# Two weight blocks of the down product loaded behind the last unit's weights: a change in the order of one DMA queue

## What is computed

```
h2 = rms_norm(x, norm_mlp[layer])
x = x + jnp.square(jax.nn.relu(h2 @ w_ff1[layer])) @ w_ff2[layer]
return rms_norm(x, norm_final)
```

## Time and profile before

| | us |
|---|---|
| median of 3 runs | 1670.12 (1668.62 to 1670.35) |
| profiled execution, its time | 1671.03 |
| its span, first to last instruction | 1669.4 |
| TensorE busy | 1654.0 (99%) |
| VectorE busy | 1023.4 (61%) |
| ScalarE busy | 706.4 (42%) |

### The profile page before, as it was taken

One profiled execution on the slowest core, in us unless ns is written; L12 is line 12 of the kernel. 1 busy time (PEld: TensorE's weight loads), 2 busy tenths in 40 slices (PEclk: granted clock), 3 DMA queues, 4 the chain that ended last, 5 costly groups with the idle time before them and its releaser, 6 DMA issues.

```text
span 1669.4 us, 25092 instructions
## 1 busy us (share of the span) xinstructions
PE 1654.0 (99%) x10242; PEld 1244.0 (75%) x10242; DVE 1023.4 (61%) x1347; ACT 706.4 (42%) x891; POOL 111.0 (7%) x168
## 2 busy tenths in 40 slices
PE   9999999999999999999999999999999999999998
PEld 7898898864444535453588877778888889889986
DVE  6975668452242334324668755567675477878887
ACT  6565553321011101111366633444542367856775
POOL 4000000000000000000011022311000001000000
PEclk9999999999999999999999999999999999999999
DMA  7233224958999999999541331223253349767864
GB/s 266 64 116 111 76 77 151 389 207 344 428 429 428 429 428 428 429 428 428 203 153 55 101 101 57 72 77 128 102 178 104 111 132 261 162 177 224 205 140 125
DMA packets 92209, 355.65 MB, mean 213 GB/s; under 512 B 7936, under 2 KB 7952, under 8 KB 79824
## 3 DMA queue, kind: packets, MB, share of 16 engines
q1 hardware_dynamic: 79776, 328.04, 50.9%
q0 software_dynamic: 12336, 26.23, 8.1%
HBM read 347.97 MB, written 6.29 MB: 212 GB/s over the span
## 4 chain that ended last, share of the span: by engine, by line
PE 95%; DMA 2%; DVE 1%; ACT 1%; issue 1%; POOL 0%; DVEq 0%; ACTq 0%; POOLq 0%
PE bank L3424 35%; PE bank L3829 13%; PE bank L4281 9%; PE bank L3842 6%; PE bank L4256 6%; PE bank L3572 6%; PE bank L3736 4%; PE bank L3775 3%; PE bank L4012 2%; PE bank L3449 2%; DMA ring<-in_w 1%; PE bank L3470 1%; DMA stage<-in_w_ff 1%; PE bank L4042 1%; PE bank L4065 1%; PE bank L4112 1%
## 5 line engine op out<-in xcount | busy, mean ns | idle before, releaser
L3424 PE MATMUL bank<-act_hi,w_hi 128*128 128x512 f32 x608 | 240.3, 395 | 0.0
L3424 PE MATMUL bank<-act_hi,w_lo 128*128 128x512 f32 x608 | 236.8, 390 | 0.0
L3424 PE MATMUL bank<-act_lo,w_hi 128*128 128x512 f32 x608 | 236.8, 389 | 0.0
L3829 PE MATMUL bank<-ring,xgT 128*64 128x512 f32 x992 | 216.1, 592 | 1.6 <-DMA ring<-in_w 1.0
L3829 PEld LDWEIGHTS bank<-ring,xgT 128*64 128x64 f32 x992 | 71.9, 137 | 141.9 <-issue 139.6
L2238 DVE TENSOR_TENSOR w_lo<-w_stage,w_hi 128x2048 fp32r<-128x2048 f32 x55 | 126.0, 2291 | 83.0 <-ACT w_hi L1324 77.2
L1324 ACT ACTIVATE w_hi<-w_stage 128x2048 fp32r<-128x2048 f32 x53 | 101.7, 1919 | 152.0 <-PE bank L3424 143.3
L4281 PE MATMUL bank<-down,part_hi 128*128 128x512 f32 x448 | 138.2, 390 | 0.2 <-issue 0.2
L3424 PEld LDWEIGHTS bank<-act_hi,w_hi 128*128 128x128 f32 x608 | 114.2, 188 | 25.8 <-issue 2.9
L3424 PEld LDWEIGHTS bank<-act_hi,w_lo 128*128 128x128 f32 x608 | 114.1, 188 | 24.3
L3424 PEld LDWEIGHTS bank<-act_lo,w_hi 128*128 128x128 f32 x608 | 114.3, 188 | 22.7
(11 more groups left out here) (584 smaller groups left out, 3585.3 us busy)
## 6 DMA issues: line engine op xcount, KB each, us to landing
ring<-in_w SPq DMA_DIRECT2D x93, 2048.0 KB, 16.6
w_stage<-in_w_in SPq DMA_DIRECT2D x40, 1024.0 KB, 5.1
w_stage<-in_w_ff SPq DMA_DIRECT2D x19, 1024.0 KB, 6.8
b_sum<-in_w_ff POOLq DMA_DIRECT2D x12, 1024.0 KB, 11.9
w_stage<-in_w_out SPq DMA_DIRECT2D x8, 1024.0 KB, 5.1
b_one<-in_w_ff SPq DMA_DIRECT2D x6, 1024.0 KB, 7.4
stage<-in_w_ff SPq DMA_DIRECT2D x5, 1024.0 KB, 5.9
x_tm<-in_x SPq DMA_DIRECT2D x8, 512.0 KB, 8.8
```

Source lines behind the costliest of these rows:

```text
L3424: ins = pe.matmul(banks[j][:, :], left, right, start=(kc == 0 and k == 0 and n_pass == 0), stop=(kc == g.chunks - 1 and k == g.ktiles - 1 ...
L3829: ins = pe.matmul(dst[mine, :], xgT[:, 4 * kh + k, slots], up_weights(2 * w + kh, q, k, ahead), start=(kh == 0 and k == 0), stop=(kh == 1 ...
```

## The change

One call in SP's program, `load_ones(0)`, which issues the loads of `b_one[1]` and of `b_far` for the first half, moves from in front of both weight blocks of unit 3 to behind them:

```diff
             load_blocks(2, 1)
             unit_split(1)
-            load_ones(0)
             load_blocks(3, 0)
             third_made(2)
             load_blocks(3, 1)
+            load_ones(0)
             unit_split(2)
             load_step(0, 0)
```

## The result

The changed kernel takes 1683.21 us (median of 6 runs, 1682.2 to 1683.41), the kernel before 1669.72 us (6 runs, 1668.62 to 1670.35): 13.5 us more, a ratio of 1.0079 with a 95% interval of 1.0069 to 1.0089. The profiled execution has a span of 1680.6 us against 1669.4 us.

What follows compares the result with a forecast made beforehand. The prediction took TensorE, busy 1654.0 of 1669.4 us, as the bound. A removed wait, a new stop and a slower clock gave -0.9 + 12.3 + 2.2 = +13.6 us, so 1683.7 us, range 1677.5 to 1688.0.

Steps and rivals of the forecast that it cites:

- The wait that comes: At product (2, 4): ScalarE stands at b_one's negation and TensorE stops; +12.3 us, or 7.6 to 16.3 us by the bounds.
- 1.95 us to spare: Before the change, slack between the low part's end at 1396.98 and TensorE's start of product (2, 4) at 1398.93.
- The time to land: b_one's load, from its issue at 1395.00 to landing at about 1407: 12 us, bounds 7.3 and 16.0 us.
- The wait that goes: At product (3, 2): TensorE's late start from late block (3, 1) should go, with less loaded ahead; -0.9 us.
- I find no other gain: Beyond the 0.87 us at product (3, 2), nothing: down-phase transfers come later and TensorE shows no wait for them.
- The clock: After the stop, product (2, 4) should begin at half rate; +2.2 us, between nothing and 2.9 us.
- The long stop: Rival: b_one waits behind (3, 1) while a third addition takes its half; stop 16.3 us, time 1688.4 us; chance 10%.
- The short stop: Rival: b_one lands 7.3 to 9.6 us after issue; stop 7.6 to 9.9 us, time 1677.9 to 1681.1; chance 18%.
- The sum: Whole kernel: -0.9 + 12.3 + 2.2 = +13.6 us, against the median of 1670.12 us makes 1683.7 us.

Runs made afterwards that it cites:

- The base run: The changed kernel run again, unaltered, beside three further variants on the same chip: 1683.26 us, ratio 1.0074 to the kernel before.

## Why the prediction was right

- **The wait that comes.** The mechanism came as forecast, and so did its size. The prediction put b_one's issue 0.41 us behind block (3, 1), its landing 12 us later and the stop at 12.3 us. The trace has 0.41, 12.1 (1393.09 to 1405.2) and 12.64 us. Its chain from there is a little short: from ScalarE's start of the negation to TensorE's first multiplication it is 1409.66 - 1405.21 = 4.45 us, not 4.2, for between the low part's end at 1409.33 and the first multiplication lie 0.33 us, where 0.05 was taken for all hand-overs. The same 0.3 us is missing in the 1.95 us to spare; but ScalarE also stood 0.29 us behind the negation for W3, which is missing too, and the two cancel. The run with the negations later shows that this stop is the whole cause, and the run with b_one alone that this load is.
- **The time to land.** That it took 12 us is a hit with luck in it. The rates of the working hold: additions alone move 196 GB/s, and beside each other the two kinds move the same number of bytes (from 1400 to 1404 in the trace of before, 0.52 MB each). Its times don't. It let block (3, 1) start 2 us after its issue and then share the engines with the second addition for 8.3 us. The first bytes came 3.9 us after the issue, at 1396.6, and the sharing ended at about 1399.5, when the addition was through; its end was worked out for 1404.7, or 1402.8 by this trace's clock, and GpSimd, which waits for it, issued the next one at 1401.40. A late start and a short sharing cancelled: block (3, 1) landed at 1402.5 against 1402.8. The sum of the working was also rounded down, as 1404.7 + 2.7 is 1407.4 and not 1407. And the base run had 13.0 us in place of 12.1, so 1 us is within what executions differ by.
- **The wait that goes.** It was taken as 0.87 us; the traces show 1.34 us. The step that failed is "I find no other gain": two further pauses hang on the late block, since they are there in both traces with 3 MB ahead of it and gone in all others. In the trace of before VectorE works without a pause from 1414.35 on and ends the low part for the first of them at 1423.18, 0.05 us before TensorE starts. The list of waits gave one of them 0.2 us "issue" and the other no row at all, and only the distance between starts shows it.
- **The clock.** 2.2 us were forecast between ends of nothing and 2.9 us. It is 1.79 us in the first trace, 1.95 in its repeat, 2.06 with b_one alone behind, and gone when TensorE works through the stop. That the clock would be down was read from rows, the 2.2 us was a choice between two ends. The upper end was too high: it took the lower level as twice the 0.12 us, and the starts are 0.21 us apart there, so that the one whole product at the lower level took 5.26 us, 2.4 us more than 2.88. The Trainium skill, page "TensorE: Matmul & The Clock Gate", section "Why this matters for your kernels", warns of idle gaps in the middle of a kernel, after which the clock falls to half; the trace agrees, with a granted clock of 0.50 from 1400 to 1406.
- **The rivals.** The long stop (16.0 us to land) didn't come in any of the traces; the longest way of b_one was 13.0 us. The short stop had a premise that came true, additions further along than worked out, and still b_one didn't land within 9.6 us, since the first bytes of block (3, 1) came so late. The Trainium skill's page "DMA: Bandwidth & Descriptors", section "Anatomy of one DMA", gives its formula for transfers that GpSimd issues, and these loads are SP's. The estimate from it, 6.8 us and a stop of 7.1 us, comes near the run with the additions cut, 7.5 us and 7.9 us, and is far from the changed kernel's 12.1 us: it has no term for the additions. The chances listed leave 3% for cases outside the range, so the 15% that it gives to the outside have no case behind them.
- **The sum.** -1.3 + 12.6 + 1.8 = 13.1 us by the traces and 13.5 by the medians, against 13.6 forecast. The three terms were off by -0.5, +0.3 and -0.4 us, so that the 0.1 us between 13.5 and 13.6 is closer than the working was.

## What to carry to other kernels

When a transfer is moved in a queue, look at what its issuer waits for between the old place and the new: passing one block of 1 MB was hidden (1670.29 against 1670.06 us), passing the wait and the block behind it was 13.5 us. Then find the instruction that consumes it, and what stands behind that on the same engine, however unrelated: here it was a negation for the next phase in front of the present phase's operands, with some 2 us to spare. If a load must come late, move its consumer too; that took back the whole loss. Then see what comes late behind it in the queue: here it was a load of the next phase, with a new pause of 0.5 to 0.9 us.

## What the runs showed of the hardware

- Transfers that add into SBUF moved half of what plain loads did: 196 GB/s with the engines' share at 1.11, against 396 with loads at 1.05. While both ran, from 1400 to 1404 in the trace of before, each moved 256 packets and 0.52 MB, but the additions held the engines for 70.4% of the time and the loads for 39.2%.
- A load of 1 MB had its first bytes moved 1.1 us after its issue with the additions cut, and 3.9 us after it while a whole addition ran. With what the additions took of the engines after that, they made 5.5 us of b_one's 13.0.
- SP's issue of a load took 0.37 to 0.70 us in the trace of before, and 1.36 and 1.44 us for the second and third of three in a row while additions held the engines. When the additions were cut these were 0.51 and 0.51 us.
- Coming back from a stop, TensorE ran 18 multiplications at the slower pace of 0.21 us in one trace, 19 in its repeat, and all 24 of a product after the stops of 7.9 and of 8.9 us (5.26 us in place of 2.88 in the first of the two). A shorter stop wasn't cheaper in clock: 2.4 us after 7.9 us, 1.8 and 1.95 us after 12.6 and 13.5 us.
